# Attention's later queries in a band of 256 keys and in classes of equal residue by 4, and gates read from their banks

## What is computed

```python
DILATED_PATTERNS = ((128, 1), (512, 4), (2048, 16))
# query t attends to keys t - j*dilation, j = 0..window//dilation
s = jnp.einsum('bhrnqd,bhrnkd->bhrnqk', qb, kw) * (Dh ** -0.5)
s = s - slopes * (dist * dilation)
s = jnp.where(valid, s, NEG_INF)
m = jnp.max(s, axis=-1); p = jnp.exp(s - m[..., None]); l = jnp.sum(p, axis=-1)
o = jnp.einsum('bhrnqk,bhrnkd->bhrnqd', p, vw) / l[..., None]
# the three patterns are joined with the weights l * exp(m - m_all)
y_b = dilated_attention(q, k, v) * jax.nn.silu(b_gate)
```

## Time and profile before

| | us |
|---|---|
| median of 3 runs | 2342.35 (2342.25 to 2343.04) |
| the profiled execution, span from first to last instruction | 2340.6 |
| PE busy | 2329.6 |
| DVE busy | 1317.0 |
| ACT busy | 867.4 |
| POOL busy | 821.3 |

### The profile page before, as it was taken

One profiled execution on the slowest core, in us unless ns is written; L12 is line 12 of the kernel. 1 busy time (PEld: TensorE's weight loads), 2 busy tenths in 40 slices (PEclk: granted clock), 3 DMA queues, 4 the chain that ended last, 5 costly groups with the idle time before them and its releaser, 6 DMA issues.

```text
span 2340.6 us, 30041 instructions
## 1 busy us (share of the span) xinstructions
PE 2329.6 (100%) x11126; PEld 1938.0 (83%) x11126; DVE 1317.0 (56%) x1831; ACT 867.4 (37%) x1308; POOL 821.3 (35%) x542
## 2 busy tenths in 40 slices
PE   9999999999999999999999999999999999999999
PEld 7888888888888888888888888888888888888887
DVE  6445764854444442247845445577787787752435
ACT  5422323233333331233444223455555555541112
POOL 3322222355555533322555454422222222223322
PEclk9999999999999999999999999999999999999999
DMA  3111222242222252223222323432332332353233
GB/s 142 43 44 37 95 85 99 81 153 81 81 81 81 81 172 98 81 99 117 108 77 72 115 97 108 171 108 81 116 125 83 105 108 90 108 189 126 91 116 117
DMA packets 70448, 238.02 MB, mean 102 GB/s; under 512 B 8432, under 2 KB 12752, under 8 KB 70224
## 3 DMA queue, kind: packets, MB, share of 16 engines
q1 hardware_dynamic: 53984, 180.55, 23.3%
q10 hardware_dynamic: 16368, 56.15, 6.0%
HBM read 177.41 MB, written 59.24 MB: 101 GB/s over the span
## 4 chain that ended last, share of the span: by engine, by line
PE 98%; DVE 1%; DMA 0%; issue 0%; ACT 0%; SPq 0%; DVEq 0%; ACTq 0%
PE dense L842 19%; PE dense L844 18%; PE dense L843 18%; PE dense L1034 10%; PE dense L1036 10%; PE dense L1035 10%; PE aux L1176 3%; PE aux L1189 1%; PE aux L1161 1%; PE aux L1188 1%; PE aux L1160 1%; PE aux L1123 1%; PE aux L988 1%; PE aux L866 0%; PE dense L1260 0%; PE dense L1262 0%
## 5 line engine op out<-in xcount | busy, mean ns | idle before, releaser
L730 POOL TENSOR_TENSOR w_lo<-w_raw,w_hi 128x512 fp32r<-128x512 f32 x246 | 388.8, 1601 | 982.2 <-ACT w_hi L1296 973.2
L842 PE MATMUL dense<-x_hi,w_hi 128*128 128x512 f32 x1424 | 578.8, 406 | 0.4 <-DVE x_lo L1893 0.4
L844 PE MATMUL dense<-x_hi,w_lo 128*128 128x512 f32 x1424 | 556.9, 391 | 0.0
L843 PE MATMUL dense<-x_lo,w_hi 128*128 128x512 f32 x1424 | 556.6, 391 | 0.0
L1296 ACT CAST w_hi<-w_raw 128x1024 fp32r<-128x1024 f32 x121 | 127.2, 1051 | 540.8 <-PE dense L844 525.9
L844 PEld LDWEIGHTS dense<-x_hi,w_lo 128*128 128x128 f32 x1424 | 267.4, 188 | 57.6
L770 POOL TENSOR_TENSOR w_lo<-w_sums,w_hi 128x512 fp32r<-128x512 f32 x144 | 227.9, 1592 | 229.0 <-ACT w_hi L1462 228.9
L842 PEld LDWEIGHTS dense<-x_hi,w_hi 128*128 128x128 f32 x1424 | 268.1, 188 | 46.2 <-issue 1.7
L843 PEld LDWEIGHTS dense<-x_lo,w_hi 128*128 128x128 f32 x1424 | 268.7, 189 | 43.3
L1034 PE MATMUL dense<-x_hi,w_hi 128*128 128x512 f32 x576 | 225.9, 392 | 1.1 <-DVE work L2223 0.9
L1035 PE MATMUL dense<-x_lo,w_hi 128*128 128x512 f32 x576 | 224.4, 390 | 0.0
(11 more groups left out here) (301 smaller groups left out, 3932.0 us busy)
## 6 DMA issues: line engine op xcount, KB each, us to landing
w_raw<-weights SPq DMA_DIRECT2D x163, 512.0 KB, 4.1
w_raw_b<-weights SPq DMA_DIRECT2D x34, 512.0 KB, 4.4
kept_qkv<-work ACTq DMA_DIRECT2D x24, 512.0 KB, 2.8
kept_m<-work ACTq DMA_DIRECT2D x22, 512.0 KB, 2.7
work<-kept_m SPq DMA_DIRECT2D x22, 512.0 KB, 3.3
residual<-xT SPq DMA_DIRECT2D x16, 512.0 KB, 6.5
kept_x<-residual ACTq DMA_DIRECT2D x16, 512.0 KB, 2.6
att_q<-kept_qkv SPq DMA_DIRECT2D x32, 256.0 KB, 4.0
```

Of the source, the lines that this page charges most:

```text
L730: last = pool.tensor_tensor(WL[:, u.slot, at4], WR[:, u.slot, at4], WH[:, u.slot, at4].bitcast(f32), ALU.subtract)
L842: pe.matmul(dst, WH[:, u.slot, k], hi, start=(k == 0), stop=False)
L843: pe.matmul(dst, WH[:, u.slot, k], lo, start=False, stop=False)
L844: last = pe.matmul(dst, WL[:, u.slot, k], hi, start=False, stop=(k == nk - 1))
```

## The change

For late queries the scores are now made in two parts of eight chunks per head, each of 128 queries by 256 keys. Chunks 0 to 3 are classes: the 128 late queries of residue n by 4 against the 256 keys of the same residue, so that Q and K are read with a step of four elements. Chunks 4 to 7 are the band: a block of 128 queries against its own keys and the 128 before. Two tables say which distance is counted in which part; they are cut at the start from `dist` and `logm` (14 DMAs, two memsets and five operations on POOL) and kept in DRAM. P is normalized in place and turned in 16 transposes per head; V gets a second split form VCL by class, from eight more transposes per pair (c0, c1), and class results are written to bank 3 by class; the band's P is read with the step of four so that its results land in the same order. `o_out` puts the order right when it writes `att_y`.

Row minima and sums of both parts (LATE) lie in different orders of partitions. `swap_stats` on SP writes both to DRAM, waits, and reads them back in the other's order: 2 writes and 5 reads per head. DVE u0 takes the smaller minimum and the two gaps, ACT x their exp, DVE u1 the shares, and DVE j0 to j7 multiply P by them.

The copy z is gone: tanh (a) and the gate's product (m) read the dense unit in its bank and free it. head_bias moves from even to odd stages. The order of the steps is new.

```diff
 PE_STEPS = [
-    "t0/t1//o0 t2/s0/o1 t3/s1/o2 t4/s2/o3 t5/s3/o4 t6//o5 t7/o6/o7 v0 v1",
-    "s0//s1/s2/t0/s3/s4/s5 o0 t1//s6/s7 o1 t2///o2 t3//o3",
+    "//s0//s1/t0/s2/t1//o0 t2/s3/o1 t3//o2//o3 v0 v1",
+    "s0/s1/s2/s3/t0 s4/s5/s6 o0 t1/s7//o1 t2//o2 t3//o3 c0/c1/",
 ]
 ACT_STEPS = [
-    "O p0 k p1 w p2 p3 e0 p4 e1 a p5 e2 p6 e3 d p7",
-    "v0 v1 O e0 w p0 e1 p1 a e2 p2 y e3 p3 q d",
+    "k x c1 O w e0 e1 p0 e2 p1 a e3 p2 d p3",
+    "v0 v1 O w e0 e1 e2 p0 e3 e4 e5 p1 e6 a e7 p2 q p3 y d c0",
 ]
 DVE_STEPS = [
-    "O l0 k l1 b l2 r0 z l3 r1 n0 l4 r2 n1 l5 r3 n2 l6 m n3 l7",
-    "v0 r0 v1 O r1 r2 z l0 r3 r4 n0 l1 r5 n1 m r6 r7 l2 n2 l3 n3 q",
+    "u0 c1 k u1 r0 j0 j1 r1 j2 j3 O l0 r2 j4 j5 j6 j7 l1 r3 n0 n1 m l2 n2 n3 l3",
+    "v0 r0 v1 r1 O r2 r3 l0 r4 r5 r6 l1 r7 m l2 q b l3 c0",
 ]
-ACT_REST = "X1 X2 O p0 X3 p1 X4 p2 X5 w p3 X6 p4 X7 p5 p6 p7"
-DVE_REST = "X1 O p0 X2 p1 X3 p2 X4 p3 X5 p4 X6 p5 X7 z p6 p7"
+PE_REST = "/////t0/t1//o0 t2//o1 t3//o2//o3//".split("/")
+ACT_REST = "X1 x X2 O X3 w p0 X4 p1 a X5 p2 X6 p3 X7"
+DVE_REST = "X1 u0 X2 u1 j0 j1 X3 j2 j3 O l0 X4 j4 j5 j6 j7 l1 X5 l2 X6 l3 X7"
+LATE_BLOCKS = ((0, 1, 3, 0), (1, 2, 4, 0), (3, 1, 7, 3)), ((0, 2, 5, 1), (2, 2, 6, 2))
...
+            def swap_stats(pair, h):
+
+                sp.wait_ge(ttr, pair.count(24, steps_before(2 * h + 1) + 8))
+                sp.wait_ge(ex, pair.count(24, steps_before(2 * h + 1) + 8))
+                for side in range(2):
+                    sp.dma_start(d_stat[side], LATE[:, 0, 8 * side:8 * side + 8]).then_inc(stat_moved, 16)
+                sp.wait_ge(stat_moved, pair.count(224, 112 * h + 32))
+                sp.dma_start(LATE[:, 1, 8:16].rearrange("p (b t) -> p b t", t=2),
+                             d_stat[0].rearrange("(b a) (r t) -> (a r) b t", b=4, t=2)).then_inc(stat_moved, 16)
+                for b in range(4):
+                    sp.dma_start(LATE[32 * b:32 * b + 32, 1, 0:8].rearrange("a (r t) -> a r t", t=2),
+                                 d_stat[1].rearrange("(a r) (b t) -> b a r t", r=4, t=2)[b]).then_inc(stat_moved, 16)
...
                 load(Unit(U_ATT + 2, j, 4))
                 load(Unit(U_ATT + 3, j, 4))
+                swap_stats(Pair(0, j), 0)
                 load_v(j + 1, False)
                 load_mixed(j)
                 load_qk(j + 1, 0, False)
                 load(Unit(U_ATT + 4, j, 4))
                 load(Unit(U_ATT + 5, j, 4))
+                swap_stats(Pair(0, j), 1)
...
             for k in range(KT):
                 if k == 3:
                     sp.wait_ge(s_ready, 24 * PAIRS)
+                    swap_stats(Pair(PAIRS - 1), 1)
...
+                if sb and n < 4:
+                    q = by_class(QS[:])[:, n, P:2 * P]
+                    hi, lo = (by_class(t[:])[:, n] for t in (KH, KL))
+                else:
+                    keys = slice((n - 1) * P if sb else 0, (n + 1) * P)
+                    q, hi, lo = QS[:, n * P:(n + 1) * P], KH[:, keys], KL[:, keys]
+                dst = PA[:, bank, 0:2 * P if sb else (n + 1) * P]
+                pe.matmul(dst, q, hi, start=True, stop=False)
+                pe.matmul(dst, q, lo, start=False, stop=True).then_inc(s_ready, 1)
...
+                elif k < 2:
+                    for b in range(4):
+                        r = 2 * k + b // 2
+                        for p in (PH, PL):
+                            last = pe.matmul(PA[:, 3, r * P:(r + 1) * P], VCL[:, h, 2 * r + b % 2],
+                                             p[:, k % 2, b * P:(b + 1) * P],
+                                             start=(k == 0 and b == 0 and p is PH), stop=False, skip_group_check=True)
+                else:
+                    for at, n, i, b in LATE_BLOCKS[k - 2]:
+                        for p in (PH, PL):
+                            last = pe.matmul(class_rows(PA[:, 3])[:, :, 32 * b:32 * (b + n)], VHL[:, h, i],
+                                             by_class(p[:, k % 2, at * P:(at + n) * P]),
+                                             start=False, stop=False, skip_group_check=True)
...
+            def late_gaps(pair, m):
+
+                h = m // 2
+                dve.wait_ge(stat_moved, pair.count(224, 112 * h + 112))
```

More of the change, by code:

```diff
@@ L541, in _ @@
                 sp.dma_start(RAW_UP[r * RANK:(r + 1) * RANK], gate_up).then_inc(tab_in, 16)
-            loads(4, 20)
+            sp.wait_ge(tab_step, 2)
+            for table, classes, src in ((DIST_ALL, DIST_CLASS, dist), (LOGM_ALL, LOGM_CLASS, logm)):
+                sp.dma_start(table[:, 0:HALF], src[:, HALF:S]).then_inc(tab_moved, 16)
+                sp.dma_start(table[:, HALF:6 * P], src[:, 6 * P:S]).then_inc(tab_moved, 16)
+                for x in range(4):
+                    sp.dma_start(classes[32 * x:32 * x + 32, 0:640 + P * x],
+                                 src.rearrange("(a r) n -> r a n", r=4)[0, :, 384 - P * x:S]).then_inc(tab_moved, 16)
+            loads(4, 6)
+            sp.wait_ge(tab_step, 7)
+            for n, t in enumerate((DIST_ALL, LOGM_ALL)):
+                sp.dma_start(d_tab[n], t).then_inc(tab_moved, 16)
+            loads(10, 14)
             sp.wait_ge(o_mm, GLA_HEADS)
@@ L797, in stage @@
                 if m == 1:
-                    pool.wait_ge(gated, pair.count(2, 1))
+                    pool.wait_ge(evac, pair.unit(0).count(1))
                     pool.wait_ge(mx_in, pair.count(16, 16))
@@ L803, in gate_y @@
                 pool.wait_ge(yh, pair.count(4, 4))
[L804 removed]
+                pool.wait_ge(evac, pair.unit(1).count(1))
                 pool.tensor_tensor(Y[:], Y[:], SBG[:], ALU.mult).then_inc(yb_up, 1)
@@ L1171, in turn_p @@
                     if m == 0:
-                        pe.wait_ge(v_lo, pair.count(2, 2))
+                        pe.wait_ge(v_lo, pair.count(4, 2))
                 if k >= 1 + sb:
-                    pe.wait_ge(pl, pair.count(24, base + k - sb))
-                for b in range(max(0, k - 4 * sb), 4):
-                    last = pe.transpose(PA[:, bank, b * P:(b + 1) * P], PBS[sb][:, b, k * P:(k + 1) * P],
-                                        IDN[:])
+                    pe.wait_ge(pl, pair.count(16, base + k - sb))
@@ new lines, in turn_p @@
+                if sb and k < 2:
+                    for b in range(4):
+                        last = pe.transpose(PA[:, bank, b * P:(b + 1) * P],
+                                            PB1[:, 2 * k + b // 2, b % 2 * P:(b % 2 + 1) * P], IDN[:])
+                elif sb:
+                    for at, (b, now) in enumerate(LATE_TURNS[k - 2]):
+                        last = pe.transpose(PA[:, bank, at * P:(at + 1) * P], PB1[:, 4 + b, now * P:(now + 1) * P], IDN[:])
+                else:
+                    for b in range(k, 4):
+                        last = pe.transpose(PA[:, bank, b * P:(b + 1) * P], PB0[:, b, k * P:(k + 1) * P], IDN[:])
@@ L1192, in stage @@
+                last.then_inc(pv, 1)
             def stage(pair, m, before=None, **have):
                 def between(g):
-                    for kind, n in steps(PE_STEPS[m % 2][g], before=bool(before), first=m == 0):
+                    for kind, n in steps(PE_STEPS[m % 2][g], before=bool(before), m=m, v_at=V_TURNED):
                         if kind == "s":
@@ L1767, in stage @@
                     act.wait_ge(sp_mx[3], 32)
-                for kind, n in steps(ACT_STEPS[m % 2], bool(before), bool(done), head, m < 2):
+                for kind, n in steps(ACT_STEPS[m % 2], bool(before), bool(done), head, m):
                     if kind == "e":
@@ L1805, in _ @@
                     split(Unit(U_PA + 1))
+                elif kind == "x":
+                    exp_gaps(final, 3)
+                elif kind == "a":
+                    gate(final, 3)
+                    store(final, 3)
                 elif kind == "X":
@@ L1808, in _ @@
             o_part(final, 3)
-            gate(final, 3)
-            store(final, 3)
             split(Unit(U_PA + 2))
@@ L2452, in stage @@
                     dve.wait_ge(sp_mx[3], 32)
-                for kind, n in steps(DVE_STEPS[m % 2], bool(before), bool(done), head, m < 2):
+                for kind, n in steps(DVE_STEPS[m % 2], bool(before), bool(done), head, m):
                     if kind == "r":
@@ L2464, in stage @@
                     elif kind == "b":
-                        head_bias(pair, m // 2)
+                        head_bias(*after(pair, m))
                     elif kind == "q":
```

266 lines of the change are left out of this document (166 added, 100 removed).

## The result

| | before | after |
|---|---|---|
| median of the runs, us | 2342.69 (2342.25 to 2343.08) | 2409.07 (2408.12 to 2410.14) |
| span of the profiled execution, us | 2340.6 | 2406.4 |

The ratio is 1.028 (1.027 to 1.0295): 66.4 us slower, where 24.7 were forecast. The first fence holds two lines of the page of after, the span and the busy times. They answer to the earlier trace rows.

What follows compares the result with a forecast made beforehand. The prediction took PE, busy for the whole span, to bound the kernel. It summed -31.5 (PE's saving) + 24.5 (stepped reading) + 27.7 (exchange) + 4 (end) = +24.7 us, to 2367 us, range 2312 to 2422.

Steps and rivals of the forecast that it cites:

- the wait that was to make the kernel slower: PE at s0 in even stages, waiting for k behind u0 and the exchange: 1.5 us (stage 0), 2.15 (stage 2).
- Edits with no cost, and their cover: Section pricing gates from banks, head_bias's move, y by class, queue orders and starting tables: nothing, or 1 us once.
- POOL's split has the rest of the stage: POOL's split of weights, in even stages: runs later behind ACT's w without delaying anything, no cost.
- The exchange: Late queries' sums through DRAM: 6.7 us round trip, landing late in even stages, +27.7 us (18.7 to 79).
- The step of four: PE reading K and P with a 16-byte step: taken as twice the columns' time, +24.5 us (0 to +78).
- Weights read with a step (Q by class, V by class) go at 0.11 per load already and I leave them: PE's stepped weight loads in late attention: 0.11 us per load already, no added cost.
- PE's ledger: PE's work in attention: -3.94 us a pair saved (-31.5 in all), +3.06 for stepped reading (+24.5).
- The clock: PE's granted clock, 1.00 before: its falling in the pauses would show the prediction wrong; no size given.
- The end: Last pair's swap delays the loads of kept_ya before the final units: +4 us (1 to 10).
- Gates from their banks: Dense units' copy leaves DVE, banks freed later with 4 us of cover before the next user: no cost.
- the forecast's own signs of error: Wrong if the pair is under 70.9 us, PE waits at t0 or o0 rather than s0, or PE's clock falls.

Runs made afterwards that it cites:

- e1: Changed kernel with l3 alone moved ahead of q and b in DVE's odd-stage list; 2402.39 us.
- e3: Changed kernel with the exchange left out (ones stand in for what it brings), DVE's order as changed; 2399.48 us.
- e2: Changed kernel with l3 ahead of q and b and the exchange left out; 2376.75 us.
- e11: e2 with POOL's split of weights moved later, away from DVE's u1, j0 and j1; 2357.88 us.
- e5: Changed kernel, all work kept, with new orders on DVE, ACT and SP (k and c1 before u0, l3 before q, POOL's split later); 2358.95 us.
- e9: e5 with ACT's store of kept_ya behind k, q before l3, m last, wider gaps in the last pair's lists, SP's last swap moved back; 2354.19 us.
- e12: e9 with ACT and DVE writing both parts of K in class order; 2366.15 us.
- e6: Kernel before with one part of the change alone: copy z gone, tanh and the gate's product read the banks; 2343.03 us, ratio 1.0001.

## Why the prediction was right in direction and wrong in size

The direction was right. The size was not: 24.7 us were forecast and 66.4 measured, and the wait that was to make the kernel slower is hardly there (0.8 us at s0). It comes out only in e1, once other waits are gone, so the kernel as it stands is slower for other reasons than the one given.

- **The step that failed is "Edits with no cost, and their cover".** It put at nothing that head_bias "moves to the odd stage behind r7", because DVE has time to spare over the stage, and never asked what is queued behind it. The list puts q and b ahead of l3, and PE's o3 waits for l3. A share of 55 of 70.9 us says nothing of a queue that has q (1.22, or 2.63 beside POOL), b (1.28) and l3 in a row while PE needs the last. The runs showed 27.2 us of waits there, up to 2.48 each. The price isn't that sum: moving l3 alone gave 6.7 us (e1), and 22.7 once the exchange was gone (e3 to e2).
- **"POOL's split has the rest of the stage"** in the same section looked at who waits for POOL, and not at what POOL holds up. e11 puts that at 18.9 us.
- **The exchange**: from the last exp to u0 it took 6.6 us for 6.7, and e1 shows 24.6 us of waits at s0 for 27.7. In the changed kernel as it stands this wait was nearly zero, since PE had already stopped at o3. Taking the exchange away was worth 9.6 us there and 25.6 in e1's order. The section computed the waits against a PE that stops nowhere else.
- **The step of four** was priced right: 3.45 us a pair for 3.06, nearly product for product. The factor of two itself was a middle between bounds of 0 and 9.8, so that it came out this well is luck. "Weights read with a step (Q by class, V by class) go at 0.11 per load already and I leave them" has the load wrong (0.31 instead of 0.19), but this cost nothing here, as the table above shows.
- **PE's ledger**, -31.5 and +24.5, is -0.88 a pair. e5 shows -0.50 in busy time, short waits included. 16 late transposes and the short products came out as priced: eight take 0.84 us in e9's trace, 0.11 each. What remains of the difference isn't resolved.
- **The clock** was named as a way to be wrong, and given no price. It fell behind six pauses: 0.54 us of a pair in after, where later waits take up the rest, and 1.6 in e12, where they don't.
- **The end**: +4 forecast, +12.0 measured, with waits at o3, t0 and for x there, and 6.1 even in e9.
- **Gates from their banks** at nothing: right (e6).
- Of the forecast's own signs of error two came true: the clock fell, and PE waited at t0 (7.0 us) and not at s0 for k. The pair is 78.3 and not 73.7. At o3, where PE waited most, the forecast didn't look.

e9, the best order found, is still 0.5% slower than before. PE's saving there is some 4 us by the estimate above, and short waits in the pairs and the longer end take more than that.

## What to carry to other kernels

When a step moves to another place in an engine's list, read who is next behind it in that list and what that one releases; the engine's free share is no cover. One wait can hide another, and one operand's cost another's: test the two apart and together before either is called harmless, or is given a share. Busy time holds short waits, so compare an engine's work from start to start.

## What the hardware showed unexpectedly

- After a pause of 2.48 us PE's granted clock was 0.50 for about 3 us, and products stood 0.43 apart. This followed six of eight such pauses in after; behind one of 2.31 and one of 2.48 us it stayed at 1.00, as it did in e12 behind one of 2.27. What decides between the two isn't settled here.
- DVE's operations on 128x8 and 128x16 took 1.20 to 1.26 us for 0.17, and two of 128x256 2.36 for 0.61, beside POOL's split; q took 2.63 for 1.22 beside POOL's `att_mixed`. One that reads a bank didn't lengthen.
- A weight load with a step of 16 bytes takes 0.31 us for 0.19; a moving operand of 256 columns 0.23 for 0.12; both together no more than the second alone. DVE reads a bank with the same step at no cost (423 ns for 421), while ACT's cast of K with the step takes 2040 ns for 1049, and DVE's subtraction for K 1973 for 1220.
- Reading back 1 KB by DMA in runs of 8 bytes landed 2.7 us after its issue, 4 KB in 1.9, writes of 4 KB in 1.5 (medians).
